# First normalisation of a decoder trunk: means taken out of y and of two weight slabs ahead of the last attention group

## The reference, cut to what matters

```python
def layer_norm(x, g, b):
    mu = jnp.mean(xf, axis=-1, keepdims=True)
    var = jnp.mean(jnp.square(xf - mu), axis=-1, keepdims=True)
    return ((xf - mu) * lax.rsqrt(var + LN_EPS) * g + b).astype(x.dtype)

mp, kp, vp = swa_prompt(xp, attn_w_qkv[j], attn_sinks[j], attn_w_o[j])   # ... heads @ w_o
xp = layer_norm(DEEPNORM_ALPHA * xp + mp, ln_mix_g[i], ln_mix_b[i])
fp, cp = conv_ffn(xp, buf0, ffn_w_in[i], ffn_conv_w[i], ffn_conv_b[i], ffn_w_out[i])
```

## Time and profile before

| what | value |
|---|---|
| time, median of 3 runs | 2847.81 us (2843.99 to 2848.66) |
| time of the profiled execution | 2848.38 us |
| its span | 2845.5 us |
| PE, DVE, ACT, POOL busy | 98%, 52%, 32%, 20% of the span |
| mean granted TensorE clock | 0.996 |
| attention group 3, end of its last job | 291 to 399 us |
| first matmul of ffn 0 | 400.01 us |

### The profile page before, as it was taken

One profiled execution on the slowest core, in us unless ns is written; L12 is line 12 of the kernel. 1 busy time (PEld: TensorE's weight loads), 2 busy tenths in 40 slices (PEclk: granted clock), 3 DMA queues, 4 the chain that ended last, 5 costly groups with the idle time before them and its releaser, 6 DMA issues.

```text
span 2845.5 us, 44456 instructions
## 1 busy us (share of the span) xinstructions
PE 2798.2 (98%) x18206; PEld 2694.0 (95%) x18206; DVE 1482.9 (52%) x2972; ACT 906.0 (32%) x1706; POOL 577.0 (20%) x504
## 2 busy tenths in 40 slices
PE   8999989999999999999999999999999999999998
PEld 7888879999999999999999999999999999999997
DVE  6556575444444444714446354465775444444455
ACT  5445464211111122422343433422252222212223
POOL 3334351000000002402223122111230000000031
PEclk9999999999999999999999999999999999999999
DMA  4210011111111112134566566786402111111102
GB/s 136 80 46 22 26 46 45 45 45 52 50 49 45 45 45 66 64 120 146 178 201 191 176 198 195 226 258 205 141 31 75 45 45 45 45 58 47 45 23 63
DMA packets 193434, 260.56 MB, mean 92 GB/s; under 512 B 29201, under 2 KB 151697, under 8 KB 193201
## 3 DMA queue, kind: packets, MB, share of 16 engines
q1 hardware_dynamic: 128336, 196.23, 22.2%
q10 hardware_dynamic: 64896, 61.50, 6.3%
HBM read 191.57 MB, written 68.20 MB: 91 GB/s over the span
## 4 chain that ended last, share of the span: by engine, by line
PE 91%; DVE 4%; ACT 2%; issue 1%; POOL 1%; DMA 0%; ACTq 0%; SPq 0%; POOLq 0%; DVEq 0%
PE bank L512 29%; PE bank L514 28%; PE bank L513 28%; ACT y L1102 1%; PE bank L665 1%; PE bank L644 1%; PE bank L1004 1%; DVE bank L1611 1%; PE bank L957 1%; PE bank L655 1%; PE bank L966 0%; PE bank L951 0%; PE bank L619 0%; DVE y L1618 0%; DMA raw<-in_w 0%
## 5 line engine op out<-in xcount | busy, mean ns | idle before, releaser
L512 PE MATMUL bank<-xh,wh 128*128 128x344 f32 x3600 | 1162.2, 323 | 2.7 <-DVE xl L1626 1.2
L514 PE MATMUL bank<-xh,wl 128*128 128x344 f32 x3600 | 1151.6, 320 | 0.0
L513 PE MATMUL bank<-xl,wh 128*128 128x344 f32 x3600 | 1150.8, 320 | 0.0
L512 PEld LDWEIGHTS bank<-xh,wh 128*128 128x128 f32 x3600 | 677.4, 188 | 18.3 <-issue 10.2
L513 PEld LDWEIGHTS bank<-xl,wh 128*128 128x128 f32 x3600 | 676.7, 188 | 5.1
L514 PEld LDWEIGHTS bank<-xh,wl 128*128 128x128 f32 x3600 | 677.5, 188 | 0.0
L1589 DVE TENSOR_TENSOR y<-bank,y 128x344 f32<-128x344 f32 x576 | 290.4, 514 | 214.8 <-PE bank L514 213.7
L2278 POOL TENSOR_TENSOR f_hl<-f_cv,f_hh 128x344 fp32r<-128x344 f32 x132 | 123.0, 933 | 1213.4 <-ACT f_hh L1276 1213.2
L512 PE MATMUL bank<-f_hh,wh 128*128 128x344 f32 x1056 | 340.1, 322 | 0.0
L514 PE MATMUL bank<-f_hh,wl 128*128 128x344 f32 x1056 | 337.9, 320 | 0.0
L513 PE MATMUL bank<-f_hl,wh 128*128 128x344 f32 x1056 | 337.5, 320 | 0.0
(11 more groups left out here) (228 smaller groups left out, 3401.8 us busy)
## 6 DMA issues: line engine op xcount, KB each, us to landing
raw<-in_w SPq DMA_DIRECT2D x216, 512.0 KB, 3.6
scratch_qkvg<-p_plain ACTq DMA_DIRECT2D x96, 172.0 KB, 2.7
r_s<-in_state_in SPq DMA_DIRECT2D x32, 512.0 KB, 3.8
out_state_s<-r_s ACTq DMA_DIRECT2D x32, 512.0 KB, 5.1
scratch_qkvg<-p_rot ACTq DMA_DIRECT2D x24, 344.0 KB, 3.8
xh<-scratch_heads_hi SPq DMA_DIRECT2D x12, 688.0 KB, 7.8
xl<-scratch_heads_lo SPq DMA_DIRECT2D x12, 688.0 KB, 9.6
r_cxq<-scratch_qkvg SPq DMA_DIRECT2D x32, 256.0 KB, 5.7
```

What stands on the lines that cost most here:

```text
L512: pe.matmul(out, ah, bh, start=(k == 0), stop=False)
L513: pe.matmul(out, ah, bl, start=False, stop=False)
L514: mm = pe.matmul(out, al, bh, start=False, stop=(k == n - 1))
```

## The change

The three means of the first normalisation are taken out of `y` at the begin of group 3, when the adds of group 2 are done, and the output weights of group 3 (slabs 18 and 19) have their row means removed, so that its products leave the mean at zero. POOL makes the sum of chunk t in round t of group 3 behind `add_rope(t)`. TensorE has mean(t-1) behind `turn(t-1)` in rounds 1 to 3, DVE `centre(t-2)` behind `t_lo(t-1)` in rounds 2 to 4. All means use bank 7, and `values(0)` waits for the third centring. DVE makes the row means of the two slabs at the end of group 2 (`weight_mean`) and splits the slabs' low parts in rounds 1 and 2 of group 3 instead of POOL. At the end of group 3 and the begin of ffn 0 the sums, means and centrings are gone; `squares` waits for the adds instead. Orders on DVE and ACT there are changed, the banks of the jobs from q = 8 and of the sample scores too, the copy of the sample heads moves from ACT to DVE in all groups, and POOL's splits of slabs 22 to 24 wait for `xl` of chunk 0. `K.wm` gets a place of its own with six columns.

```diff
@@ -151,7 +151,7 @@
-    mine = set(range(5, 26)) | {S_R + j for j in range(2, 6)} | {S_F1 + j for j in range(2, 6)}
+    mine = set(range(5, 18)) | set(range(20, 26)) | {S_R + j for j in range(2, 6)} | {S_F1 + j for j in range(2, 6)}
     on_pool, nth, seen = [], [], [0, 0]
@@ -213,7 +213,9 @@
         return q % 2
-    return (0, 1, 3)[(q - 8) % 3] if g == NG - 1 else (0, 1, 3, 4)[q % 4]
+    if g < NG - 1:
+        return (0, 1, 3, 4)[q % 4]
+    return q % 2 if q < 12 else {22: 5, 23: 2}.get(q, (3, 0, 1)[q % 3])
@@ -221,7 +223,7 @@
         kind = key[0]
-        if kind == "qkv" or (kind == "ao" and key[1:] < (NG - 1, 8)):
+        if kind == "qkv" or (kind == "ao" and key[1:] < (NG - 1, 12)):
             continue
@@ -311,7 +313,7 @@
-    return (3, 4) if u == 0 else (6, 7)
+    return (7, 4) if u == 0 else (7, 7) if u < 3 else (6, 7)
@@ -319,6 +321,15 @@
 S_LAST = N_SLABS - 4
+
+S_AO = 5 * NG - 2
+
+
+def row_means(s):
+
+    return s - S_LAST + 2 if s >= S_LAST else s - S_AO if S_AO <= s < S_AO + 2 else None
+
+
@@ -659,6 +670,8 @@
                 pe.wait_ge(T["heads_lo"], NB * g + b)
+            elif last:
+                pe.wait_ge(S["n_cent"], 3)
             first = 0 if b else 1
@@ -672,8 +685,8 @@
             for b in range(NS):
-                pe.matmul(bank[4][:, b:32:NS], K.a_kc[:, b, :], K.a_sq[:, 0:4, b], start=True, stop=True)
-            pe.matmul(bank[4][0:32, 32:32 + NS], K.a_sq[:, 0:4, :], K.a_sq[:, 4, :], start=True, stop=True).then_inc(T["s_sc"], 1)
+                pe.matmul(bank[3][:, b:32:NS], K.a_kc[:, b, :], K.a_sq[:, 0:4, b], start=True, stop=True)
+            pe.matmul(bank[3][0:32, 32:32 + NS], K.a_sq[:, 0:4, :], K.a_sq[:, 4, :], start=True, stop=True).then_inc(T["s_sc"], 1)
@@ -708,8 +721,8 @@
                     pe.wait_ge(T["rope_t"], (NB + 1) * g + (NB + 1 if q == 4 else NB - 1 + q))
-                if last and q == 10:
-                    pe.wait_ge(S["n_cent"], 1)
+                if last and q == 12:
+                    pe.wait_ge(T["s_scc"], 3 * g + 3)
                 if att_before(g, q) is not None:
@@ -723,6 +736,8 @@
                 turn(t - 1)
+            if last and 1 <= t <= 3:
+                mean(t - 1)
             if last and t == NB:
@@ -737,23 +752,19 @@
             turn_probs(NB - 2)
-            pe.wait_ge(T["shifted"], GH * NB * (g + 1))
-            mean(0)
             down(8, 10)
...
             down(10, 12)
+            var(0)
             turn_probs(NB - 1)
             down(12, 14)
-            var(0)
             values(NB - 1)
...
             sample_values()
-            down(16, 20)
-            mean(1)
-            down(20, 24)
+            down(16, 24)
             return
@@ -792,13 +803,11 @@
                     var(u + 1)
-                if half == 1 and (t, kind) == (0, 0):
-                    mean(u + 2)
         for t, kind in tiles[n_halved:]:
...
                 var(u + 1)
-            if (t, kind) == (0, 1):
+            if (t, kind) == (0, 1) and L == 1:
                 mean(u + 2)
@@ -1059,13 +1068,17 @@
             act.wait_ge(R["out_"], NI)
-        if s < S_LAST:
+        n = row_means(s)
+        if n is None:
             act.activation(K.wh[:, SLOT[s], :], K.raw[:, s % RAW, :], ACT.Copy).then_inc(S["hi_done"], 1)
             return
-        n = s - S_LAST
+        if n < 2:
+            act.wait_ge(S["w_mean"], 2 * n + 2)
+            act.activation(K.wh[:, SLOT[s], :], K.raw[:, s % RAW, :], ACT.Identity, bias=K.wm[:, n:n + 1]).then_inc(S["hi_done"], 1)
+            return
         act.activation(K.sq[:, :, :].rearrange("p a n -> p (a n)")[:, 0:SLAB], K.raw[:, s % RAW, :], ACT.Identity, scale=-1.0 / D,
                        accum_out=K.wm[:, n:n + 1]).then_inc(S["w_mean"], 1)
-        act.wait_ge(S["w_mean"], n + 1)
+        act.wait_ge(S["w_mean"], n + 3)
         act.activation(K.wh[:, SLOT[s], :], K.raw[:, s % RAW, :], ACT.Identity, bias=K.wm[:, n:n + 1]).then_inc(S["hi_done"], 1)
@@ -1082,10 +1095,11 @@
         c = columns(u % NCH)
-        if u < 9:
+        if 3 <= u < 9:
             act.wait_ge(S["n_cent"], u + 1)
         else:
-            act.wait_ge(S["yadd"], EV["fin", 1, KT * (u % NCH) + KT - 1][1])
+            job = KT * (u % NCH) + KT - 1
+            act.wait_ge(S["yadd"], EV[("ao", NG - 1, job) if u < 3 else ("fin", 1, job)][1])
         after(act, S["n_var"], u)
@@ -1219,24 +1233,18 @@
-        def sample_heads_hi():
-            act.wait_ge(T["s_of"], 2 * g + 2)
-            act.activation(K.a_oh[:, :, SEQ:TOK], K.a_of[:, :, :], ACT.Copy).then_inc(T["s_oh"], 1)
-
         if last:
...
             act.activation(K.warm[:, :], K.eps[:, :], ACT.Sqrt)
-            pt_in(NB - 1)
             act.wait_ge(S["g_in"], 64)
             root(0)
-            split_next(1)
+            pt_in(NB - 1)
+            split_next(2)
             heads_hi(NB - 1)
-            split_next(1)
             normal(0, 0)
-            sample_heads_hi()
             normal(0, 1)
@@ -1556,8 +1563,8 @@
         dve.wait_ge(S["hi_done"], s + 1)
-        if s >= S_LAST:
-            n = s - S_LAST
+        n = row_means(s)
+        if n is not None:
             dve.scalar_tensor_tensor(K.wl[:, SLOT[s], :], K.raw[:, s % RAW, :], K.wm[:, n:n + 1],
@@ -1702,8 +1709,8 @@
             dve.wait_ge(T["s_sc"], g + 1)
-            dve.tensor_copy(K.a_ss[:, :], bank[4][:, 0:32]).then_inc(T["s_scc"], 1)
-            dve.tensor_tensor(K.a_new[:, 0:NS], bank[4][0:32, 32:32 + NS], K.same[:, :], ALU.mult).then_inc(T["s_scc"], 1)
+            dve.tensor_copy(K.a_ss[:, :], bank[3][:, 0:32]).then_inc(T["s_scc"], 1)
+            dve.tensor_tensor(K.a_new[:, 0:NS], bank[3][0:32, 32:32 + NS], K.same[:, :], ALU.mult).then_inc(T["s_scc"], 1)
             dve.wait_ge(T["s_scc"], 3 * g + 2)
@@ -1733,7 +1740,9 @@
-        def sample_heads_lo():
+        def sample_heads_split():
+            dve.wait_ge(T["s_of"], 2 * g + 2)
+            dve.tensor_copy(K.a_oh[:, :, SEQ:TOK], K.a_of[:, :, :]).then_inc(T["s_oh"], 1)
             dve.wait_ge(T["s_oh"], g + 1)
@@ -1748,6 +1757,14 @@
                 add(("ao", g, q))
+
+        def weight_mean(s):
+
+            n = row_means(s)
+            dve.wait_ge(S[f"raw_in{s % RAW}"], 16 * (s // RAW) + 16)
+            dve.reduce_sum(K.wm[:, n:n + 1], K.raw[:, s % RAW, :], AXX).then_inc(S["w_mean"], 1)
+            dve.wait_ge(S["w_mean"], 2 * n + 1)
+            dve.tensor_scalar(K.wm[:, n:n + 1], K.wm[:, n:n + 1], -1.0 / D, None, ALU.mult).then_inc(S["w_mean"], 1)
@@ -1761,39 +1778,43 @@
                 split_lo(t - 1)
+            if last and t in (1, 2):
+                split_lo(S_AO + t - 1)
+            if last and 2 <= t <= 4:
+                centre(t - 2)
+            if last and t == NB:
+                add_y(4, 6)
             if t >= 4:
...
         if last:
-            add_y(4, 6)
             inverse(NB - 2)
...
             t_lo(NB)
+            shift(NB - 1)
             heads_lo(NB - 3)
-            shift(NB - 1)
-            centre(0)
+            sample_copy()
             inverse(NB - 1)
+            sample_shift()
             add_y(8, 10)
-            sample_copy()
-            sample_shift()
             sum2(0)
-            add_y(10, 12)
             heads_lo(NB - 2)
             sample_probs()
-            add_y(12, 13)
+            add_y(10, 12)
             inverse_root(0)
             sample_probs_copy()
-            scale(0)
+            add_y(12, 13)
+            scale(0, (0,))
             heads_lo(NB - 1)
...
             sample_heads()
-            sample_heads_lo()
+            sample_heads_split()
+            scale(0, (1,))
+            add_y(16, 18)
             normal_lo(0, (0,))
-            add_y(16, 18)
+            add_y(18, 20)
             normal_lo(0, (1,))
-            add_y(18, 20)
-            centre(1)
             add_y(20, 24)
@@ -1815,8 +1836,12 @@
         add_y(12, 14)
+        if g == NG - 2:
+            weight_mean(S_AO)
         sample_heads()
-        sample_heads_lo()
+        sample_heads_split()
+        if g == NG - 2:
+            weight_mean(S_AO + 1)
         add_y(14, 24)
@@ -1872,7 +1897,8 @@
         scale(u + 1)
-        centre(u + 2)
+        if L == 1:
+            centre(u + 2)
         normal_lo(u + 1)
@@ -2228,27 +2254,21 @@
             if t >= 3:
-                if t == NB + 1 and g == NG - 1:
-                    sums(key, 0, 0, 4, 6)
-                if t == NB + 2 and g == NG - 1:
-                    sums(key, 0, 0, 6, KT)
                 probs(t - 3)
...
                 add_rope(t)
-            if t == NB and g == NG - 1:
-                sums(key, 0, 0, 1, 4)
+            if t < NCH and g == NG - 1:
+                sums(lambda q: ("ao", NG - 2, q), 0, t, 1, KT)
         if g < NG - 1:
             for s in range(5 * g + 5, 5 * g + 10):
-                split_lo(s)
+                if LO_POOL[s]:
+                    split_lo(s)
         else:
-            sums(key, 0, 1, 1, 5)
             split_lo(20)
```

(12 more changed lines are left out.)

## The result

The changed kernel takes 2881.07 us (median of 4, 2879.54 to 2883.64) against 2848.23 us for the kernel before on the same chip: ratio 1.0117, 95% interval 1.0104 to 1.0129. It is slower by 32.8 us; the forecast was 24.

What follows compares the result with a forecast made beforehand. TensorE, busy 98% of the span, was taken as the bound. Begin of group 3 +33.0, group 2's end 0, end of group 3 -8.5: +24.5 on 2848.4, predicted 2872 us; range 2856 to 2885, own spread 2864 to 2879 (0.58).

Steps and rivals of the forecast that it cites:

- the four waits: Begin of group 3: TensorE waits before mean(0), mean(1), mean(2) and values(0), 6.7 + 6.8 + 5.5 + 5.5 = 24.5 us.
- The first sum: Begin of group 3: GpSimd's seven adds behind add_rope(0) take 7.4 us plus 1.2 disturbance, ending at 306.6; mean(0) waits 6.7.
- The clock: Lower TensorE clock behind each of the begin's four waits: 1.7 us each, 6.8 in all (bounds 0 and 17).
- (a): End of group 3: the 1.7 wait before down(6,8) goes; a wait of 1.3 at values(5) takes its place.
- (b): End of group 3: the 1.9 before mean(0) goes; down(8) waits about 2.2 for heads_lo(5) behind shift(7), starting 0.5 earlier.
- (c): End of group 3: down(10) waits about 1.4, var(0) 1.0; down(16) starts about 383.3 behind 2.6 instead of 4.9.
- (d): From down(16) to ffn 0: eight jobs run to 390.9, against ffn 0's first matmul at 400.01 before; gain so far 9.1.
- (e): Begin of ffn 0: var(1) waits 1.0 for sum2(1); clock +1.6 and -1.7, mean(2) gone +0.6; end's gain taken as 8.5.
- C: Rival: the clock stays low between the begin's waits, from mean(0) to values(0), +11.4, 2883 us; chance 0.14.
- A: Rival, faster: the begin's means find sums and centrings ready and cost only their matmuls, 2841 us; chance 0.06.
- B: Rival: waits as forecast, but the clock costs 0 to 2 and the end gives 12 to 17, 2860 us; chance 0.16.
- D: Rival: no change within 0.2%, begin at its lower end and group 3's end at its upper, 2853 us; chance 0.06.

Runs made afterwards that it cites:

- no_means: The changed kernel without the three sums, means and centrings at the begin of group 3: 2842.26 us, ratio to before 0.9983.
- sum_early: The changed kernel with GpSimd's sum of chunk 0 ahead of add_rope(0): 2871.35 us, ratio to before 1.0086.
- spread: The changed kernel with the same sums, means, centrings and splits moved to where their engine is idle and inputs ready: 2848.40 us, ratio to before 1.0002.
- fill_waits: The changed kernel with spare matmuls, results unused, ahead of the four waits at the begin of group 3: 2871.19 us, ratio to before 1.0087.
- heads_first: The spread kernel with heads_lo(5) ahead of shift(7) again, as before the change: 2843.08 us, ratio to before 0.9986.
- changed_heads: The changed kernel with only heads_lo(5) ahead of shift(7) again: 2876.52 us, ratio to before 1.0106.
- squares_first: heads_first with squares(1) ahead of ScalarE's splits of slabs 22 and 23, and GpSimd's splits of 22 to 24 waiting for sum2(1): 2847.30 us, ratio 0.9998.
- before_fill: The kernel before the change with spare matmuls in its own waits at the end of group 3: 2847.53 us, ratio 1.0000.
- spread_fill: The spread kernel with spare matmuls in three waits of the last stage, before down(8), q = 10 and q = 16: 2845.55 us, ratio to before 0.9994.

## Why the prediction was right, and where it was short

**The direction and the four waits: right, and nearly to the size.** Forecast 6.7, 6.8, 5.5, 5.5 (24.5 us); measured 6.0, 6.5, 6.4, 5.3 (24.2) beside the earlier trace rows. The chain of the third wait in VectorE's timeline of the changed kernel, rope of the round, then t_lo, then the centring:

```profile
329.88 0.49 DVE L1658 TENSOR_TENSOR a_t<-bank,cosT 128x320 f32<-128x320 f32 x1 [6.87 <-ACT a_v L1161]
...
333.72 0.41 DVE L1666 TENSOR_TENSOR a_ql<-bank,a_qh 128x256 fp32r<-128x256 f32 x1
...
334.25 3.00 DVE L1606 TENSOR_TENSOR y<-y,bank 128x2752 f32<-128x2752 f32 x1
```

The projection ended at 329.5, the rope starts 0.4 later, the centring ends 7.7 after the projection's end, and mean(2) starts 7.9 after it, at 337.40. The forecast had 6.85. In the next round it fits: the projection ends at 345.66, values(0) starts 6.8 later, at 352.42. In this round two small steps of shift took 0.80 and 0.65 where 0.16 and 0.17 stand in the next, while GpSimd ran probs and add_rope beside them; that this is the reason was not tried. no_means and sum_early show that these waits are the cause, not only that they are there.

**The first sum.** GpSimd in the changed kernel, the answer to the earlier trace rows:

```profile
298.39 0.73 POOL L2240 TENSOR_TENSOR a_qk<-a_t,a_t 128x256 f32<-128x256 f32 x1 [14.73 <-DVE a_t L1660]
...
299.50 0.93 POOL L2281 TENSOR_TENSOR n_ms<-y 128x344 f32<-128x344 f32 x1
300.57 6.97 POOL L2284 TENSOR_TENSOR n_ms<-n_ms,y 128x344 f32<-128x344 f32 x6
307.81 0.72 POOL L2240 TENSOR_TENSOR a_qk<-a_t,a_t 128x256 f32<-128x256 f32 x1 [0.27 <-POOL n_ms L2284]
```

The first add and the six grouped behind it run from 299.50 to 307.54; mean(0) starts at 307.65. Add_rope(0) starts right behind rope(0), 2.7 ahead of turn(0) where it was 2.3 in before, as forecast, and seven adds take 8.0 against the forecast's 7.4 undisturbed: 0.6 of disturbance where 1.2 was taken. VectorE's split beside it took 1.71 instead of 1.30. By the Trainium skill (SBUF — State Buffer, Who interferes with whom) a VectorE instruction with two SBUF inputs contends with a GpSimd instruction that reads SBUF, it is the order of issue that decides who is blocked, and a `tensor_reduce` on trn2 never contends. The runs agree: the split and sum2(1) suffered, and the weight mean did not, 1.21 with GpSimd's split of slab 17 beside it and 1.21 without (VectorE, changed kernel):

```profile
282.40 1.21 DVE L1765 TENSOR_REDUCE row_means<-raw 128x1 f32<-128x1024 f32 x1
...
284.40 1.21 DVE L1765 TENSOR_REDUCE row_means<-raw 128x1 f32<-128x1024 f32 x1
...
302.97 1.71 DVE L1568 SCALAR_TENSOR_TENSOR wl<-raw,row_means,wh 128x1024 fp32r<-128x1024 f32 x1
```

GpSimd's split beside the first of these two reductions:

```profile
281.29 2.37 POOL L2227 TENSOR_TENSOR wl<-raw,wh 128x1024 fp32r<-128x1024 f32 x1 [2.67 <-ACT wh L1073]
```

**Means: right** (1.7; spread shows 0.6 for each). **Group 2's end: right.** The weight means took 1.21 and 0.15 each, and all of it was hidden: no wait of TensorE ends behind them in group 2, and no_means, which has them, has the begin of before. **Shares moved at no cost** (banks, the sample heads' copy): nothing in the runs speaks against it.

**The clock: the term that was mis-sized, twice.** The forecast took one value, 1.7 us per low stretch, from one place. Behind the four waits the lower level lasted 5.2, 3.6, 6.1 and 4.7 us of matmuls, 9.8 lost instead of 6.8. At the end the forecast charged one low stretch, 1.7 behind the wait before down(16); it came, 1.6. But the forecast has no term for the stretch near the sample tokens' scores (from 369 us in before, 1.7 lost). Here it began ahead of these scores, at 401.6, behind the waits of 1.2 and 2.3, held through their small matmuls and one more wait of 1.3, and lost 6.2 in 13.6 us. So the end lost 7.7 where 1.7 was charged. The clock cost 17.5 - 5.1 = +12.4 instead of 6.8 + 1.7 - 5.1 = +3.4 (+5.1, if the forecast is read as leaving the stretch at 369 as it was). These 9.0 us, less 0.3 and 1.2 by which the waits of the begin and of the end were shorter than forecast, make 7.5 of the 10.3 between 24.5 and the span's 34.8. Another 1.6 lie ahead of turn(0), where the trace has low stretches that before has not; 1.2 stay without a term. fill_waits confirms the begin's part by removing it alone (9.5 less between the marks). The size at the end is not explained: the same order lost 4.0, 5.9, 5.9, 7.7 and 7.8 in five kernels, one execution each, and the stretches at 86 and 178 us (or 270) show that the same instructions can lose 3.4 us or none. The Trainium skill (TensorE: Matmul & The Clock Gate, HAM oscillation — how this bites in real kernels) says of a kernel with a wait in each round that it pays the restart each time; four of four did so here.

**End of group 3, by steps.** (a) The 1.7 went and values(5) waits 1.2 (forecast 1.3): right. (b) The wait before down(8) is 2.3 (2.2): right, and heads_first and changed_heads show its cause, the order of heads_lo(5) and shift(7): 0.4 in both. (c) q = 10 waits 1.3 (1.4), var(0) not at all (1.0), q = 16 1.8 (2.6): TensorE ran at half speed here and came later to each; in no_means and fill_waits, which lost less, q = 10 waits 2.0. (d) So ffn 0 began 3.1 earlier by the marks, not 9.1. This is the step of the forecast that failed, and the clock is its main part: the waits up to there were 6.6, less than the 8.5 forecast, while the clock lost 7.7. (e) var(1) waits 1.7 instead of 1.0; its cause was missed, GpSimd's splits beside sum2(1) (squares_first). Two of the forecast's signs came out wrong with this: ffn 0's first matmul is 34 us later than 400, not 24 to 25, and the time ahead of turn(0) and behind ffn 0's begin moved by 2.2, where the bound for the time outside the stage was 2. The measured 2881 lies outside the forecast's own spread (2864 to 2879) and inside its range only because that was drawn wide enough to take in most of C.

**Rivals.** A fell (a wait of 5 us or more at each of the four places); its mechanism is real, though: spread has the inputs ready and pays 1.2. B and D fell. C, the clock staying low between the waits, is the nearest to the measured time (2883), but its mechanism isn't what happened: full speed came back in each round, the low stretches were only longer, and two thirds of the clock's excess (6.0 of 9.0) lie at the end of the group. That its time comes closer than the forecast's own is chance. B's argument, that the waits of 1.9 and 1.7 of before cost one low stretch, reads that stretch wrongly: before_fill fills the 1.9 and loses the same 1.7.

## What to carry to other kernels

Where an in-order engine waits for a result of another one, look at what stands ahead of the producer in that other queue: if this needs the waiting engine's own last step, the whole chain is paid each round, whatever the busy shares say. Work moved to an earlier, idle stage must be cut to the holes of every engine that it touches; the same work cost 35.7 us in one place and under 2 in another. A wait of TensorE has a second price at the lower clock, here 0.4 us for each us waited in the begin, and it should be ranged by several stretches of a trace, not by one, and by more than one execution.

## What the runs showed of the hardware

- The granted clock came back to 1.00 after 3.6 to 6.1 us of matmuls at 0.50 behind waits of nearly equal length (5.3 to 6.5), so one measured stretch does not give the price of the next.
- Spare matmuls into an unused bank kept the clock at 1.00 through waits of 5 to 6 us (fill_waits). Started after the clock had fallen, they ran at half speed, and the kernel's time stayed as it was (before_fill, ratio 1.0000).
- The clock also fell with no wait beside it: in spread_fill at about 369 us, with TensorE busy for all of the windows from 366 to 374, behind 16 small matmuls (64x4). And in the same instructions at 86 to 91 and 178 to 183 us the changed kernel's trace lost 3.4 us to it, that of before none.
- VectorE's sum of 128x688 took 0.88 alone and 2.94 beside GpSimd's splits (four in 11.4 us); its reduction of 128x1024 took 1.21 with a GpSimd split beside it and 1.21 without.
